# A 16-head delta-rule stage inside a hybrid decoder layer: keys turned earlier, block-wise solver levels, a transpose in place of a product

## The reference, cut to what matters

```python
gc = jnp.cumsum(g, axis=-1)
decay_strict = jnp.where(strict, exp(gc_i - gc_j), 0.0)
a_mat = jnp.einsum('bhncd,bhnjd->bhncj', k * beta, k) * decay_strict
sol = lax.linalg.triangular_solve(a_mat + eye, rhs, left_side=True, lower=True, unit_diagonal=True)
qk = jnp.einsum('bhncd,bhnjd->bhncj', q, k) * decay_incl
# then per chunk: u = value - k_cum @ S;  o = q_dec @ S + qk @ u;  S = S * g_last + k_dec^T @ u
```

## Time and profile before

| | |
|---|---|
| median of 3 runs | 3637.98 us (3637.32 to 3639.64) |
| the profiled execution | 3641.78 us, its span 3640.0 us |
| PE busy in the span | 3081.8 us (85%) |
| DVE, ACT, POOL busy | 1726.0, 651.2, 534.2 us |
| loop over heads, iterations 1 to 14 | 741.4 us of the span |
| granted TensorE clock | 0.842 over the span |

### The profile page before, as it was taken

How to read it: one execution, slowest core, us unless ns; L and a number is a source line. 1 busy time by engine, 2 the same in 40 slices (tenths; PEclk the granted TensorE clock), 3 DMA queues, 4 the chain that set the end, 5 groups by cost and what they waited for, 6 DMA issues and landing times.

```text
span 3640.0 us, 48806 instructions
## 1 busy us (share of the span) xinstructions
PE 3081.8 (85%) x17428; PEld 2053.9 (56%) x17428; DVE 1726.0 (47%) x4236; ACT 651.2 (18%) x1771; POOL 534.2 (15%) x625
## 2 busy tenths in 40 slices
PE   8989999999998999999999999888655666666565
PEld 7766777777776699998888888655200000000000
DVE  4496555555555200017333333468844444444544
ACT  1002323323332100011111111121212111111112
POOL 1000111211111000003111111113311111111111
PEclk9999999999999999999999999989755555555555
DMA  5343333333342688878999999999999999999998
GB/s 220 139 136 136 124 103 123 124 121 122 123 128 79 239 298 291 296 255 315 419 409 420 408 409 413 420 420 408 390 419 413 422 423 424 422 422 424 417 423 361
DMA packets 159446, 1097.42 MB, mean 301 GB/s; under 512 B 22948, under 2 KB 66084, under 8 KB 72892
## 3 DMA queue, kind: packets, MB, share of 16 engines
q0 software_dynamic: 46080, 671.11, 44.0%
q1 hardware_dynamic: 106236, 403.18, 31.1%
q10 hardware_dynamic: 7024, 21.70, 1.5%
HBM read 1064.19 MB, written 31.67 MB: 301 GB/s over the span
## 4 chain that ended last, share of the span: by engine, by line
PE 57%; DMA 23%; DVE 11%; issue 6%; ACT 2%; POOL 1%; DVEq 0%; ACTq 0%; POOLq 0%; SPq 0%
PE psum L558 30%; DMA kv<-in_peer_uv,idx 19%; PE psum L647 13%; PE psum L1037 5%; DVE kv L2045 2%; DVE branches L1530 2%; DMA kv<-in_peer_uv,shared 1%; PE psum L721 1%; PE psum L712 1%; PE psum L718 1%; DMA branches<-in_peer_uv,shared 1%; PE psum L1015 1%; DMA ring_mm<-in_w_outp 1%; DVE ring_mm L2045 1%; DVE ring_mm L1685 1%
## 5 line engine op out<-in xcount | busy, mean ns | idle before, releaser
L558 PE MATMUL psum<-hT,ring_mm 128*128 128x128 f32 (+2 forms) x4736 | 793.4, 328 | 24.8 <-DMA ring_mm<-in_w_glu 11.4
L558 PEld LDWEIGHTS psum<-hT,ring_mm 128*128 128x128 f32 x4736 | 709.8, 195 | 101.0 <-issue 33.2
L1015 PE MATMUL psum<-shared,selb 32*128 32x512 bf16 x1280 | 300.0, 525 | 415.7 <-DVE dots L2045 415.4
L647 PE MATMUL psum<-hT,ring_mm 128*128 128x320 f32 x2112 | 621.8, 434 | 0.0
L1015 PEld LDWEIGHTS psum<-shared,selb 32*128 32x128 bf16 x1280 | 55.5, 96 | 979.8 <-DVE dots L2045 880.7
L2045 DVE CUSTOM_DVE_ANT_0 ring_mm<-ring_mm,psum 128x1024 f32<-128x1024 f32 x320 | 377.9, 1218 | 375.8 <-DMA ring_mm<-in_peer_uv,idx 247.9
L647 PEld LDWEIGHTS psum<-hT,ring_mm 128*128 128x128 f32 x2112 | 379.5, 190 | 137.5 <-issue 15.5
L1365 ACT ACTIVATE ge<-dots 128x1 f32<-128x1 f32 x320 | 94.3, 295 | 1346.0 <-DVE dots L2045 1337.2
L558 PE MATMUL psum<-branches,ring_mm 128*128 128x128 f32 (+1 forms) x2048 | 292.8, 301 | 1.2 <-issue 1.2
L2045 DVE CUSTOM_DVE_ANT_0 kv<-kv,psum 128x1024 f32<-128x1024 f32 x160 | 189.0, 1218 | 208.1 <-DMA kv<-in_peer_uv,idx 119.4
L558 PEld LDWEIGHTS psum<-branches,ring_mm 128*128 128x128 f32 x2048 | 283.4, 191 | 4.7 <-issue 4.7
(11 more groups left out here) (445 smaller groups left out, 2753.8 us busy)
## 6 DMA issues: line engine op xcount, KB each, us to landing
ring_mm<-in_w_merge SPq DMA_DIRECT2D x160, 1024.0 KB, 5.2
ring_mm<-in_w_head SPq DMA_DIRECT2D x64, 1024.0 KB, 6.2
ring_mm<-in_w_outp SPq DMA_DIRECT2D x32, 1024.0 KB, 8.8
ring_mm<-in_w_pq SPq DMA_DIRECT2D x32, 1024.0 KB, 9.6
ring_mm<-in_w_att SPq DMA_DIRECT2D x24, 1024.0 KB, 7.7
ring_mm<-in_w_mem SPq DMA_DIRECT2D x16, 1024.0 KB, 6.3
ring_mm<-in_w_glu SPq DMA_DIRECT2D x16, 1024.0 KB, 5.7
out_qkv_out<-ring_mm ACTq DMA_DIRECT2D x16, 520.5 KB
```

The source lines that it names most:

```text
L558: last = mat(out, ring[:, j, (k0 + kt) * P:(k0 + kt + 1) * P], src[:, kt, :], start=kt == 0, stop=kt == kts - 1)
L647: last = mat(ps[j][:, 0:TOKENS], ring[:, j, kt * P:(kt + 1) * P], hT[:, kt, :], start=kt == 0, stop=kt == KT - 1)
L1015: last = mat(ps[q][:, :], selb[32 * q:32 * q + 32, j, :], hb[32 * q:32 * q + 32, g_, :], start=True, stop=True)
```

## The change

The keys' transposes and the keys' Gram matrix move ahead of all fills of the iteration, and the sums of squares and the four `kscale` operations move to the end of the iteration before (ScalarE and VectorE, ahead of the norm's root and reciprocal there). The query products get their own place after nine fills. VectorE makes I - lt0 itself in two operations, and GpSimd makes four masks in place of seven. At levels 1 to 4 `tn` is no longer updated by a product and a subtraction: the updated `tt` is turned by TensorE and copied. At levels 5 and 6 only the blocks that are not zero are computed, as products with 32-column weights and 32 or 64 columns of data, straight from `at3`. ScalarE decays `sin` in eight parts at levels 3 to 6 in place of GpSimd. The fills are spread anew (their sum stays 64). `warm` and `hs_pool` go.

```diff
 LEVELS = [1, 2, 4, 8, 16, 32, 64]
-HEAD_STEPS = 32
-TOP, LEVEL_P, LEVEL_D = 12, 2, 2
+HEAD_STEPS = 33
+KEYS_TO_QUERIES, QUERIES_TO_TURN = 9, 4
+LEVEL_FILL = [(), (2, 2, 2), (2, 2, 2), (2, 2, 2), (2, 1, 1), (2, 2), (2, 2)]
 SAMPLE_LEVELS = 3
+MASKED = 5
+def halves(l):
+    s = LEVELS[l]
+    return [(slice(b, b + s), slice(b + s, b + 2 * s)) for b in range(0, P, 2 * s)]
+def quarters(r):
+    return [slice(b, b + 32) for b in range(r.start, r.stop, 32)]
...
-                fill(TOP + 5)
...
                 last.then_inc(k_turned, 1)
-                pe.wait_ge(q_ready, h1)
-                pe.wait_ge(o_done, h)
-                for n, src in enumerate((kn, qn)):
-                    for u in range(UNITS):
-                        c = slice(u * P, (u + 1) * P)
-                        last = mat(ps[4 + n][:, c], kn[:, c], src[:, c], start=True, stop=True)
+                pe.wait_ge(orm_ready, h)
+                for u in range(UNITS):
+                    c = slice(u * P, (u + 1) * P)
+                    last = mat(ps[4][:, c], kn[:, c], kn[:, c], start=True, stop=True)
                 last.then_inc(g_done, 1)
...
                 last.then_inc(tok_done, 1)
-                fill(7)
+                fill(KEYS_TO_QUERIES)
+                pe.wait_ge(q_ready, h1)
+                pe.wait_ge(o_done, h)
+                    last = mat(ps[5][:, c], kn[:, c], qn[:, c], start=True, stop=True)
+                last.then_inc(g_done, 1)
+                fill(QUERIES_TO_TURN)
...
-                    pe.wait_ge(lt_ready, len(LEVELS) * h + l + 1)
+                    if l < MASKED:
+                        pe.wait_ge(lt_ready, LT * h + l)
...
+                    else:
+                        for lo, hi in halves(l):
+                            for r in quarters(hi):
+                                for u in range(units):
+                                    last = mat(three(4)[r, u, lo], at3[:, u, r], tn[:, u, lo], start=True, stop=True)
-                    fill(LEVEL_P)
+                    fill(LEVEL_FILL[l][0])
-                    if l < len(LEVELS) - 1:
+                    if l < MASKED:
                         for u in range(units):
-                            last = mat(ps[5][:, u * P:(u + 1) * P], tt[:, u, :], pm[:, u, :], start=True, stop=True)
+                            last = mat(ps[6][:, u * P:(u + 1) * P], pm[:, u, :], tt[:, u, :], start=True, stop=True)
+                    else:
+                        if l < len(LEVELS) - 1:
+                            lo, hi = halves(l)[0]
+                            for u in range(units):
+                                last = mat(three(5)[hi, u, lo], tt[:, u, hi], pm[:, u, lo], start=True, stop=True)
+                            last.then_inc(dd_done, 1)
+                        for lo, hi in halves(l):
+                            for r in quarters(lo):
+                                for u in range(units):
+                                    last = mat(three(6)[r, u, hi], pm[:, u, r], tt[:, u, hi], start=True, stop=True)
+                        last.then_inc(dd_done, 1)
...
-                    fill(LEVEL_D)
+                    fill(LEVEL_FILL[l][1])
+                    if l < MASKED:
+                        pe.wait_ge(t_ready, T_STEPS * h + 2 * l + 1)
+                        for u in range(units if l + 1 < SAMPLE_LEVELS else 2):
+                            last = nc.tensor.transpose(ps[5][:, u * P:(u + 1) * P], tt[:, u, :], ident[:])
+                        last.then_inc(dd_done, 1)
+                        fill(LEVEL_FILL[l][2])
...
-                fill(1)
+                fill(5)
...
-                fill(2)
+                fill(4)
...
-                fill(3)
+                fill(2)
...
+            def decay_states(h, batches):
+                act.wait_ge(ks_done, 2 * h + 1)
+                for b in batches:
+                    last = fn(sin[:, b, :], sin[:, b, :], ACT.Copy, scale=hs[:, EGLB + b:EGLB + b + 1])
+                if b == NBATCH - 1:
+                    last.then_inc(sc_done, 1)
...
+                    else:
+                        for lo, hi in halves(l):
+                            last = fn(pm[hi, 0:units, lo], three(4)[hi, 0:units, lo], ACT.Copy)
+                    last.then_inc(p_ready, 1)
+                    if l > 2:
+                        decay_states(h, range(2 * (l - 3), 2 * (l - 2)))
                     if nxt is not None:
-                        if l == 2:
-                            window(nxt, 1)
-                        if l == 5:
+                        if l == 4:
+                            window(nxt, 1)
+                        if l == 6:
...
                     query_squares(nxt)
-                    fn(warm[:], ones[:, 0:1], ACT.Sqrt)
+                    key_sums(nxt)
                 act.wait_ge(orm_ready, h1)
...
+                dve.wait_ge(sc_done, h)
...
+                dve.wait_ge(at_ready, h1)
+                st(v.tensor_tensor(tt[:, :, :], at3[:, :, :], lm[:, 0, :].unsqueeze(1).to_broadcast([P, UNITS, P]), ALU.mult))
+                st.wait()
+                v.tensor_tensor(tt[:, :, :], ident[:].unsqueeze(1).to_broadcast([P, UNITS, P]), tt[:, :, :], ALU.subtract)\
+                    .then_inc(t_ready, 1)
+                dve.wait_ge(g_done, 2 * h + 2)
...
-                dve.wait_ge(lt_ready, len(LEVELS) * h + 1)
-                v.tensor_tensor(tt[:, :, :], ident[:].unsqueeze(1).to_broadcast([P, UNITS, P]),
-                                lt[:, 0, :].rearrange("p (u n) -> p u n", u=UNITS), ALU.subtract).then_inc(t_ready, 1)
                 dve.wait_ge(turn_done, h1)
                 v.tensor_copy(tn[:, :, :], three(4)).then_inc(t_ready, 1)
...
-                    if l < len(LEVELS) - 1:
+                    if l < MASKED:
-                        v.tensor_tensor(tn[:, 0:units, :], tn[:, 0:units, :], three(5)[:, 0:units, :], ALU.subtract)\
-                            .then_inc(t_ready, 1)
+                        v.tensor_tensor(tt[:, 0:units, :], tt[:, 0:units, :], three(6)[:, 0:units, :], ALU.subtract).then_inc(t_ready, 1)
+                        n = units if l + 1 < SAMPLE_LEVELS else 2
+                        dve.wait_ge(dd_done, 11 * h + 2 * l)
+                        v.tensor_copy(tn[:, 0:n, :], three(5)[:, 0:n, :]).then_inc(t_ready, 1)
+                    else:
...
-                        if l == 3:
+                        if l == 4:
                             convolve(nxt, 1, range(2))
-                        if l == 4:
+                        if l == 5:
...
                     decays_in(nxt)
+                    keys_scaled(nxt)
                 dve.wait_ge(ort_ready, h1)
...
-                pool.wait_ge(at_ready, h1)
-                for l in range(len(LEVELS)):
+                pool.wait_ge(t_ready, T_STEPS * h + 1)
+                for l in range(1, MASKED):
...
-                pool.wait_ge(so_done, h1)
-                g.tensor_tensor(sin, sin, hs_pool[:, EGLB:EGLB + NBATCH].unsqueeze(2).to_broadcast([P, NBATCH, P]),
-                                ALU.mult).then_inc(sc_done, 1)
```

67 lines of the change are left out of this document (36 added, 31 removed).

## The result

| | before | changed |
|---|---|---|
| median of 5 runs each | 3637.98 us (3635.00 to 3639.64) | 3611.40 us (3605.81 to 3618.56) |
| profiled execution, its span | 3641.78, 3640.0 | 3611.40, 3609.4 |
| granted TensorE clock over the span | 0.842 | 0.842 |
| 14 heads, norm sum to norm sum | 741.2 us, 52.95 a head | 719.0 us, 51.36 a head |

What follows compares the result with a forecast made beforehand. TensorE's stream plus its waits bounds a head. Work -1.22 + 0.1 and waits -0.44 made -1.56, less 0.25 given back, -1.3 a head; 14 x -1.3 - 3 = -21 us, median 3617 us, range 3604 to 3634.

Steps and rivals of the forecast that it cites:

- likeliest case: Whole kernel: the forecast gain of 0.8 to 2.0 us a head, 3606 to 3627 us, chance 0.66.
- Bound: Loop over heads: a head costs what TensorE streams, some 50.0 us, plus waits of 2.94 us.
- Levels 1 to 4, -1.22 of work and +0.75 of waits: Transposes replace products, 11 passes fewer, -1.22 us a head; two new waits at level 4, 0.4 and 0.35 us.
- Levels 5 and 6, +0.1: Ten products of 2.22 us a head become 18 small ones in four groups, taken at 2.3 us.
- a small pass costs as much as a full one: Rival for levels 5 and 6: 36 passes at 0.111 us, +1.2 us a head, about 3657 us, chance 0.06.
- a floor of 0.06 a pass: Rival for the small groups: an instruction floor makes them take 3.3 us; 3628 to 3631 us, chance 0.07.
- The front, +0.47: Start of a head: new waits of 1.0 and 0.75 us take the place of the 1.28 at the turn of `tt`.
- a front that becomes a VectorE chain of longer hops: Rival at the front: slower hops and slipping transitions at levels 1 to 3 lose 1.2 us a head; 3634 us, chance 0.14.
- The tail, -1.66: End of a head: the waits at L749 (1.13 us) and L764 (0.53 us) both go.
- Give-back of 0.25 a head: Levels 1 and 2: cover of three transitions only equals the chain within 0.1 us, so 0.25 us is returned.
- The ends: First head gains 3 us, lacking two front waits; last head gains 0, some 1.2 us more front wait eating its gain.
- What would show it: Signs in the trace: head of 51.4 to 51.9 us, small groups 0.4 to 0.7 us each, `o_done` within 10 us of L796.

Runs made afterwards that it cites:

- products_back: Changed kernel with levels 1 to 4 updating `tn` by a product and a subtraction again, not transpose and copy: 3627.08 us, 0.9966.
- gpsimd_decays: Changed kernel with the decay of the sampled states back on GpSimd as one operation behind the last products: 3622.87 us, 0.9960.
- window_early: Changed kernel with the next head's window load ahead of the wait for the state store in SyncE's queue: 3609.65 us, 0.9909.
- level4_fills: Changed kernel with fills 2, 2, 2 at level 4 for 2, 1, 1, and 4 and 3 in the tail for 5 and 4: 3600.55 us.
- double_blocks: Changed kernel with the small products of level 6 issued twice: 3619.55 us, 0.9937.
- norm_window: Changed kernel with the norm's root ahead of the key squares and the window load ahead of the state store's wait: 3588.47 us, 0.9858.
- before_tail_window: Kernel before with the change's tail alone, plus the second projection tile's window copy and convolution moved later as in the change: 3624.41 us, 0.9954.
- norm_first: Changed kernel with key squares behind the norm's root on ScalarE and scale operations behind the norm's last product on VectorE: 3609.78 us, 0.9920.
- before_tail: Kernel before with only the change's tail: ScalarE decays the states, five fills moved from the top to the tail: 3640.26 us, 1.0003.

## Why the prediction was right

The forecast said 3617 (3604 to 3634), and faster with a chance of 0.80; it came out at 3611.4, and by its likeliest case. By its steps:

- **Bound.** Right: a head is TensorE's stream plus its waits. Where a run took work off TensorE or a wait away from it (products_back, gpsimd_decays), the head followed; where it took only another engine's wait away (window_early), nothing moved.
- **Levels 1 to 4, -1.22 of work and +0.75 of waits.** Right in kind, and 0.31 too careful. Level 4 less its fills takes 1.72 us where level 3, with the same passes and no wait, takes 1.15, so its waits (with the way into the small form beneath them) are 0.57, and the work of the four levels is down by 0.78 + 0.57 = 1.35. Of the 0.57 only 0.22 went when level4_fills took the two waits away, so the waits alone were charged at 0.75 and cost 0.22. products_back gives 1.00 for the exchange of products against transposes.
- **Levels 5 and 6, +0.1: the mis-sized term.** The small groups were to take 2.3 us, 1.2 of stream and four switches of 0.28; levels 5 and 6 hold 1.70 of it, and the 20 full passes had taken 2.27. The switch of 0.28 agrees with double_blocks (0.28 to 0.32). The stream is smaller, some 0.77 to 0.85 (16 passes at 0.030, 20 at 0.015 to 0.019), near the 0.7 that I had for a full overlap of column groups; which passes overlap no run shows. And one of the four switches lies in level 4 under a wait, so three are left here. The rivals "a small pass costs as much as a full one" and "a floor of 0.06 a pass" fell with the 0.030.
- **The front, +0.47.** Measured +0.68, some 0.53 without the border's share. The two new waits came as forecast, 1.03 and 0.84 for 1.0 and 0.75. (By its own terms the forecast should have had TensorE ready at 8.6 and 14.2, not 8.5 and 14.15, and so waits of 0.9 and 0.7.) norm_window confirms their main cause, the root behind the squares: 1.33 a head goes with it. The rival of a front that becomes a VectorE chain of longer hops did not come: `o_done` came 9.7 us after L796, against the 10 set as its mark.
- **The tail, -1.66.** Both waits went, and the stretch gained only 0.96, the head some 0.81. Two things were missed. First, a new wait of 0.33 at L778 (0.19 by its matmuls). Second, the size: an idle time of the weight loads is not all lost time, since the matmuls of the last fill still stream. For L749 the weight loads showed 1.13 and the matmuls 0.62; for L764 0.53 and none. With L778 that bounds the gain between 0.43 and 1.33. The starts of the weight loads divide it, with the fills taken out. From L746 to L752 it was 1.19 (747.23 to 750.02, three fills) and from L778 to L784 it is 0.32 (729.17 to 734.30, nine fills): L749's wait of 1.13 cost 0.86. From the fills ahead of the norm sum to the first behind it, it was 0.68 (752.10 to 754.38, three fills) and is 0.38 (736.39 to 737.84, two fills): L764's 0.53 cost 0.30. From L740 to L746 it was 1.10 (746.13 to 747.23) and from L772 to L778 it is 1.46 (727.71 to 729.17): L778's wait takes 0.36 back. The sum is 0.80, and before_tail_window, with the tail alone, gains 0.82. The rows of the first pair, before and then changed:

```profile
747.23 0.30 PEld L746 LDWEIGHTS psum<-ring_mm 128*128 128x128 f32 x2
...
750.02 0.46 PEld L752 LDWEIGHTS psum<-ring_mm 128*128 128x128 f32 x2
```

```profile
729.17 0.30 PEld L778 LDWEIGHTS psum<-ring_mm 128*128 128x128 f32 x2 [0.33 <-ACT ring_mm L1233]
...
734.30 0.46 PEld L784 LDWEIGHTS psum<-ring_mm 128*128 128x128 f32 x2
```

- **Give-back of 0.25 a head.** This step was too large. What shows at levels 1 to 3 is 0.15 of idle weight loads ahead of level 2's P in each head, which starts 0.07 later than level 3's does behind its fills, and the 0.18 to 0.44 at level 1 in five heads, which the window's copy makes; without it window_early is 0.03 a head faster. The head was forecast at -1.3 and came at -1.59. Without the give-back the sum was -1.56, but it is right by cancelling, which is luck: by the stretches of the table the tail was 0.70 and the front 0.21 too good (0.85 and 0.06 without the border's share), levels 5 and 6 0.65 and levels 1 to 4 0.31 too bad.
- **The ends.** First head -3 forecast, -3.11 measured. Last head 0 forecast, -1.98 measured. The forecast charged new waits at its front (they came: 1.03, 0.27 and 1.90 for the 2.52 ahead of the old L704) and forgot that GpSimd's decay goes from its tail as well. The tail of the last head before, and then of the changed kernel:

```profile
1171.70 1.90 POOL L2170 TENSOR_TENSOR ring_mm<-ring_mm,hs_pool 128x1024 f32<-128x1024 f32 x1 [3.51 <-PE psum L754]
...
1172.12 1.82 DVE L1735 TENSOR_TENSOR mean<-mean,ring_mm 128x320 f32<-128x320 f32 x1
...
1173.99 0.30 PEld L764 LDWEIGHTS psum<-mean,ones 128*128 128x128 f32 x2 [2.15 <-DVE mean L1735]
```

```profile
1143.68 0.49 DVE L1804 TENSOR_TENSOR mean<-mean,ring_mm 128x320 f32<-128x320 f32 x1
1144.22 0.30 PEld L796 LDWEIGHTS psum<-mean,ones 128*128 128x128 f32 x2 [0.82 <-DVE mean L1804]
```

- **What would show it.** The head was to take 51.4 to 51.9 and took 51.36, just under it; the small groups 0.4 to 0.7 each and took 0.43 (a quarter of 1.70); window copies that wait for their DMA and hold the copy of P at level 1 were named as a danger. They do wait, 3.0 us, and hold it a little in five of 14 heads, and in all of them once the front is shorter (norm_first).

Open: why the prologue is up to 3 us shorter or longer from one execution to the next; which of the small passes overlap, and how a switch divides between the way in and the way out; and whether the store of the window alone makes the wait at L778. No run takes these apart.

## What to carry to other kernels

Price a wait of TensorE from both of its rows: here the weight loads' idle time was the upper bound and the matmuls' the lower (1.07 and 0.57 for a wait that cost 0.82; 1.13 and 0.62 for one that cost 0.86). When fills or other cover move, list what each in-order queue copies out of them: the piece that ends later holds whatever stands behind it, and that decided before_tail and, by the order of the queue, more than half of level4_fills. After a wait is removed, look for one that was already there on another engine and hidden by it; the load of the window was worth 0.03 us a head until the root was moved, and 1.15 thereafter.

## What the runs showed of the hardware

- **A small pass is cheap.** A pass (weight load and matmul) with 32-column weights and 64 columns of data took 0.030 us in a group of 16 (double_blocks), half of the 0.06 of the forecast's rival of a floor. In TensorE: Matmul & The Clock Gate, on the gap of 56 ns, the Trainium skill gives about 62 ns per MATMUL when instructions are not decoded in hardware; the run does not agree with that case.
- **Going into the small form and out again costs about 0.3 us:** 0.28 by double_blocks, 0.32 by the rows of level 6, and 0.36 by level4_fills; it can lie under a wait that is there anyway. The Trainium skill says in TensorEngine Tiling (Array Packing), Key Properties, that a change of the mode drains the engine; the runs agree in that each change costs time, and give its size.
- **GpSimd and VectorE hold each other up.** A VectorE operation of 256 columns went from 0.43 to 1.86 us, one of 320 from 0.49 to 1.82, beside one GpSimd operation of 1.90; both ended some 0.3 us behind it. The other way, the second GpSimd mask of 384 columns in a head (L2230) takes 1.31 beside VectorE's L1740, where the first takes 1.00. The Trainium skill names the contention for operations with two inputs in SBUF in GPSIMD Engine Reference, Key points; these rows agree.
